# Attention logits of two heads issued in one block that alternates between the row halves of TensorE

## What is computed

```python
# even layer: 8 heads of kind A (top-k selected keys), 8 heads of kind B (bias by distance)
logits = jnp.einsum('bqhd,bqkhd->bhqk', qb, k_sel) * scale          # A
logits = jnp.einsum('bqhd,bshd->bhqs', qc, kc) * scale + bias[None]   # B
# odd layer: 8 heads of kind C (forgetting), 8 heads of kind D (window, sinks, 2 key heads)
logits = jnp.einsum('bqhd,bshd->bhqs', qb, k) * scale + fq[..., None] - f_cum[:, :, None, :]
logits = jnp.einsum('bnqkgd,bnskd->bnkgqs', qb, kband) * (dh ** -0.5)
p = jax.nn.softmax(logits, axis=-1)
y = jnp.einsum('bhqs,bshd->bqhd', p, v)
```

## Time and profile before

| | |
|---|---|
| Median of 3 runs | 1335.07 us (1334.74 to 1338.38) |
| The profiled execution's own time | 1332.6 us |
| Its span, first to last instruction | 1330.8 us |
| TensorE matmuls busy | 1289.0 us, 97% |
| TensorE loads of weights busy | 1179.5 us, 89% |
| VectorE, ScalarE, GpSimd busy | 840.3, 703.6, 241.9 us |
| Mean granted clock of TensorE | 0.99 |
| DMA | 200.29 MB, mean 151 GB/s |

### The profile page before, as it was taken

The page is one execution under the profiler, slowest core; times in us unless marked ns, Lnnn a source line. Parts: engine busy times, 40 slices in busy tenths (PEclk is TensorE's granted clock), DMA queues, the critical chain, the costliest instruction groups (busy, mean ns, idle before and its releaser), DMA issues.

```text
span 1330.8 us, 21614 instructions
## 1 busy us (share of the span) xinstructions
PE 1289.0 (97%) x8824; PEld 1179.5 (89%) x8824; DVE 840.3 (63%) x1454; ACT 703.6 (53%) x1161; POOL 241.9 (18%) x196
## 2 busy tenths in 40 slices
PE   8999999999999999999999999999899999999996
PEld 7777899998877789998889999999889989999875
DVE  6774487774664458776467787778843456555445
ACT  5555466553445546654355666666646335444344
POOL 2000000000000010000046665565435201000001
PEclk9999999999999999999989999999999999999999
DMA  8523355445442245545433322332202536455432
GB/s 317 215 100 122 112 190 177 178 179 182 164 152 102 89 176 219 185 175 198 143 127 127 128 96 98 125 126 97 96 33 98 182 139 216 182 190 189 175 143 79
DMA packets 31442, 200.29 MB, mean 151 GB/s; under 512 B 4272, under 2 KB 6464, under 8 KB 8560
## 3 DMA queue, kind: packets, MB, share of 16 engines
q1 hardware_dynamic: 29360, 189.79, 39.5%
q0 software_dynamic: 1840, 8.60, 1.6%
q10 hardware_dynamic: 144, 0.52, 0.1%
HBM read 197.85 MB, written 1.05 MB: 149 GB/s over the span
## 4 chain that ended last, share of the span: by engine, by line
PE 89%; DVE 5%; ACT 3%; issue 1%; DMA 0%; POOL 0%; SPq 0%; POOLq 0%; DVEq 0%; ACTq 0%
PE ps L1019 25%; PE ps L1021 24%; PE ps L1020 24%; PE ps L1174 2%; PE ps L1377 2%; PE ps L1142 1%; PE ps L1393 1%; DVE conv L2526 1%; PE ps L1035 1%; PE ps L1155 1%; PE ps L1333 1%; PE ps L1100 1%; DVE wlo L2150 1%; PE ps L1338 1%; PE ps L1399 1%
## 5 line engine op out<-in xcount | busy, mean ns | idle before, releaser
L1019 PE MATMUL ps<-xhi,whi 128*128 128x256 f32 x1536 | 441.3, 287 | 2.6 <-DVE xlo L2233 2.6
L1020 PE MATMUL ps<-xlo,whi 128*128 128x256 f32 x1536 | 436.3, 284 | 0.0
L1021 PE MATMUL ps<-xhi,wlo 128*128 128x256 f32 x1536 | 436.2, 284 | 0.0
L2150 DVE TENSOR_TENSOR wlo<-raw,whi 128x2048 fp32r<-128x2048 f32 (+2 forms) x144 | 324.7, 2257 | 124.5 <-ACT whi L1661 121.2
L1661 ACT ACTIVATE whi<-raw 128x2048 fp32r<-128x2048 f32 (+2 forms) x144 | 270.7, 1882 | 117.0 <-PE ps L1021 112.7
L1019 PEld LDWEIGHTS ps<-xhi,whi 128*128 128x128 f32 x1536 | 296.1, 193 | 2.9 <-DVE xlo L2233 2.8
L1020 PEld LDWEIGHTS ps<-xlo,whi 128*128 128x128 f32 x1536 | 296.1, 193 | 0.1
L1021 PEld LDWEIGHTS ps<-xhi,wlo 128*128 128x128 f32 x1536 | 295.8, 193 | 0.0
L977 POOL TENSOR_TENSOR wlo<-raw,whi 128x1024 fp32r<-128x1024 f32 x72 | 173.8, 2422 | 60.8 <-ACT whi L1670 60.5
L897 POOL TENSOR_SCALAR sumsq<-sumsq 128x1 f32<-128x1 f32 x18 | 5.8, 322 | 890.5 <-ACT xn L1687 700.9
L1019 PE MATMUL ps<-whi,xhi 128*128 128x512 f32 (+4 forms) x432 | 152.2, 352 | 4.0 <-DVE xlo L2236 3.4
(11 more groups left out here) (296 smaller groups left out, 1757.4 us busy)
## 6 DMA issues: line engine op xcount, KB each, us to landing
raw<-in_stream SPq DMA_DIRECT2D x176, 1024.0 KB, 4.8
gain<-in_gains POOLq DMA_DIRECT2D x7, 512.0 KB, 5.4
bias<-in_rel POOLq DMA_DIRECT2D x1, 1536.0 KB, 8.9
raw<-in_stream SPq DMA_DIRECT2D x2, 648.0 KB, 7.9
cst<-in_consts POOLq DMA_DIRECT2D x1, 1280.5 KB, 6.2
raw<-in_stream SPq DMA_DIRECT2D x2, 528.0 KB, 4.1
x<-in_x SPq DMA_DIRECT2D x2, 512.0 KB, 4.8
out<-xn SPq DMA_DIRECT2D x2, 512.0 KB, 2.6
```

What stands on the lines that cost most here:

```text
L1019: nc.tensor.matmul(out, a_hi, b_hi, start=start, stop=False)
L1020: nc.tensor.matmul(out, a_hi, b_lo, start=False, stop=False)
L1021: return nc.tensor.matmul(out, a_lo, b_hi, start=False, stop=stop)
L2150: dve.tensor_tensor(used(wlo, n), used(raw, n), used(whi, n).bitcast(F32), ALU.subtract)\
```

## The change

At an even head's step TensorE issues the logits of this head and of the next one, tile by tile, alternating between the two heads (so between the row halves); at the next step it issues none. Each head still goes to the bank that it had, and each still signals its own `products`. Before the block TensorE waits for both banks. VectorE and ScalarE keep their steps. In the odd layer the turn of group 1 moves from behind head 10 to behind head 9, so that heads 10 and 11 are in neighbouring steps.

```diff
-         "odd": heads(0, 8) + [("mixed", 0)] + heads(8, 11) + [("mixed", 1)] + heads(11, 16)
+         "odd": heads(0, 8) + [("mixed", 0)] + heads(8, 10) + [("mixed", 1)] + heads(10, 16)
...
-                old, o = bank_before(layer, s)
-                if old == "head":
-                    pe.wait_ge(*S["logits"].at((layer, o, TT - 1)))
-                if old == "mixed":
-                    pe.wait_ge(*S["mixed_low"].at((layer, o)))
+                if what == "head" and e % 2:
+                    return
+                for at in (s, s + 1) if what == "head" else (s,):
+                    old, o = bank_before(layer, at)
+                    if old == "head":
+                        pe.wait_ge(*S["logits"].at((layer, o, TT - 1)))
+                    if old == "mixed":
+                        pe.wait_ge(*S["mixed_low"].at((layer, o)))
...
                     for t in range(TT):
-                        q, k = qk_of(kind, h, t)
-                        last = nc.tensor.matmul(ps[:, bank, tile_logits(t)], q, k, start=True, stop=True)
-                    last.then_inc(*S["products"].one((layer, e)))
+                        for a in range(2):
+                            q, k = qk_of(kind, h + a, t)
+                            last = nc.tensor.matmul(ps[:, logit_bank(layer, s + a), tile_logits(t)], q, k, start=True, stop=True)
+                            if t == TT - 1:
+                                last.then_inc(*S["products"].one((layer, e + a)))
```

## The result

The changed kernel takes 1317.14 us (median of 4 runs, 1314.96 to 1317.94) against 1334.9 of the kernel before: ratio 0.986 with a 95% interval of 0.9834 to 0.9885. The forecast was 1326.4 in a range of 1319.7 to 1333.0, so the gain is twice the one forecast and lies just beyond the rival of full overlap, (B). The profiled execution took 1317.6 us, with a span of 1315.8 against 1330.8: 15.0 us less.

The account below looks back on a forecast made before the run. The prediction took TensorE to bound both attention stretches. 16 pairs at 0.61 gave 9.8 us, with the four places 8.7, off the median 1335.07: 1326.4 us, range 1319.7 to 1333.0.

Parts of the forecast that it names:

- (B): Rival for the blocks of two heads: full overlap, gain 15.4 us, so 1319.7 us; chance 0.12.
- Taken: 1.47: Assumed TensorE time of a two-head block: only one 256-column pass overlaps, 1.47 us, gain 0.61 a pair.
- The lower end: Bound on a block's TensorE time: second head runs wholly beside the first, 1.04 us, gain 1.04 a pair.
- the four places: One spot in the even layer, three in the odd, where gain differs: +0.22, -0.15, -0.4 and -0.69 us.
- The cost of 0.40 for entry and exit: On TensorE, 0.40 of a head's 1.04 us is paid entering and leaving the 64-row form.
- the first was sized +0.22: Even layer, block of heads 8 and 9: idle time behind head 8 hides the block's extra; +0.22 us.
- the second 0.15 for 0.17: Odd layer, block of heads 8 and 9: waits for the remainders of turned group 0; -0.15 us.
- the third 0.4 for 0.18: Odd layer, moved group 1: block of heads 10 and 11 waits for its remainders on VectorE; -0.4 us.
- the fourth 0.69 for 0.85: Odd layer, last block: TensorE meets head 13's probability copy; gains 0.20, then 0.15 at the next copy; -0.69 us.
- (A): Rival for the blocks: no overlap, only ends saved, 5.6 us, so 1329.5 us; chance 0.18.
- (C): Rival: changing row halves inside a block drains TensorE; 13 us slower, so 1348 us; chance 0.10.
- (D): Rival: TensorE's gain partly lost to more waits, 5 of 8.7 us, so 1331.4 us; chance 0.12.

Follow-up runs that it names:

- e2_in_turn: The changed kernel with both tiles of the block's first head issued before both of the second, instead of alternating; 1319.32 us, ratio 0.9876.
- e3_same_half: The changed kernel with both products of a block reading the even head's operands, so both in rows 0 to 63; 1328.01 us, ratio 0.9945.
- e8_full_rows: The kernel before, with the logits' products over all 128 rows instead of 64 (a different result); 1320.0 us, ratio 0.9894.
- e4_order_only: The kernel before, with only the odd layer's group 1 turned behind head 9 instead of head 10; 1333.71 us, ratio 0.9995.
- e5_last_single: The changed kernel with the last two heads of the odd layer issued singly, as before; one execution, 1319.71 us.
- e9_changed: The changed kernel unaltered, run again beside an extended kernel on one chip; 1318.15 us, ratio 0.9871 to the kernel before.
- e7_both: The changed kernel plus ScalarE's early copy of v (even layer) and the indexer's products alternating between row halves; 1313.43 us, ratio 0.9842.
- e10_both_again: The kernel of e7_both again, beside e9_changed on one chip; 1315.64 us, ratio 0.9852 to the kernel before.

## Why the prediction was wrong

**The step that failed is the price of the block, "Taken: 1.47".** It measured 1.06, a gain of 1.02 a pair where 0.61 was counted. All three assumptions behind it were carried over from one head, and the runs contradict the two that mattered. "Loads follow each other at 0.107" is true within a half only: eight loads of two halves span 0.52, not 0.86. "Matmuls start in program order" is false across halves: with head after head in the block, the fifth pass starts 0.01 us behind the first (e2_in_turn). Only "one half can't hold two running passes" stands (e3_same_half, 1.50). A row that shows pacing in one resource was used as a bound on two resources. The lower end that I gave, 1.04, is within 0.02 of the truth, and I had set the load pace against it.

**The rest of the sum was right or small.** With 1.06 in place of 1.47 it is 16 x 1.02 = 16.3, less 1.2 for the four places: 15.1, against 15.0 in the spans and 15.3 in the stages. TensorE as the bound of both stretches: right; nothing took its place. The cost of 0.40 for entry and exit, and that it belongs to the form: right, 0.38 in e8_full_rows and 0.38 in e3_same_half. Of the places, the first was sized +0.22 and is nothing beside a full 1.04 (head 8's end did not move); the second 0.15 for 0.17; the third 0.4 for 0.18, since TensorE came to the block some 0.2 later than I had it, and the splitting and the remainders took 2.88 together where I had added 2.29 and 0.69 (VectorE began the splitting 1.63 behind the values' end, as I had it); the fourth 0.69 for 0.85: the 0.15 counted at the second copy did not come.

**Rivals.** (B) is what happened, and I gave it 0.12. The Trainium skill ("TensorE: Matmul & The Clock Gate", Part 3) had it: one matmul's duration and about 4 ns for a second row group; the trace agrees (0.93 for 0.92). I had doubted that rule because another remark of the same part is contradicted by the rows, which was no reason against the rule. (A) is excluded by the block's 0.93, and is what e3_same_half looks like: its stages give 5.4 us over the kernel before, where (A) had 5.6. (C) is excluded: three changes of half inside a block cost nothing that shows (0.93 for 0.92). The Trainium skill ("TensorEngine Tiling (Array Packing)", Key Properties) says that a change of mode drains TensorE and a change of tile alone doesn't; the trace agrees. (D): of the waits for banks that were moved, two are visible, 0.35 us together, where (D) had 5.

**The median.** 15.0 us are accounted for in the profiles; the medians differ by 17 to 18. The mean granted clocks of the executions say where the rest lies. Span times clock is an estimate of the time without the lower level (it takes all of the span as following the clock): on average 1317.3 us over 40 executions of the kernel before and 1302.8 over 16 of the changed one, 14.4 less. What is left of the span, the estimate of what the lower level costs, is 16.2 before and 13.0 after, 3.2 less with a standard error of 0.9. So by this estimate some 3 us of the 17 to 18 come with the clock and 14 to 15 with the work. Why the changed kernel lost less to the clock is open.

## What to carry to other kernels

Products of 64 rows between products of 128 cost TensorE an entry and an exit, here 0.38 us together, so gather them in blocks; and put partners from the two row halves into the same block, where the second one is all but free (0.02 us), in either order tried here. The partners wrote to different banks of PSUM in every run; whether the same bank would do was not tried. Bound an unseen overlap with the full overlap as a live case, and don't let the pace of one half stand for both. Behind the shorter stage look at who waits next: here the order of two pieces of work on ScalarE held 2.0 us.

## What the runs showed of the hardware that I had not expected

The two halves behave as if each had its own stream of loads and matmuls: 8 loads of two halves lie in 0.52 us and 8 two-pass fp32 matmuls in 0.93, in either order; of one half they take 1.17 and 1.57 (e3_same_half).

Eight of the profiles have an idle stretch of TensorE of 2.1 us (2.07 to 2.16) ahead of the even layer's output projection. Behind it the clock went to the 1.2 GHz level in three: for about 7 us in e4_order_only (3.1 us lost) and for about 3.4 us in e5_last_single and e9_changed (1.6 us lost in each). In the other five, the kernel before and the changed kernel among them, it stayed up behind the same stretch. This place is not the larger part of the scatter. In every profile the clock also fell for some us between 650 and 710 us and again between 940 and 1060 us, and two executions of the same kernel, e7_both and e10_both_again, need 852.45 and 860.08 us from the norm behind the odd layer to the end.
